# Three instead of four ordinary pairs ahead of the Strassen pairs in each feed-forward of a hybrid backbone step

## The reference, cut to what matters

```python
def swiglu(h, w_in, w_out):
    g, u = jnp.split(h @ w_in, 2, axis=-1)
    return (jax.nn.silu(g) * u) @ w_out

def trunk_layer(x, cond, ...):
    mod = (jax.nn.silu(cond) @ w_mod + b_mod)[:, None, :]
    sh1, sc1, g1, sh2, sc2, g2, sh3, sc3, g3 = jnp.split(mod, N_MOD, axis=-1)
    h = rms_norm(x, norm_pre[0]) * (1.0 + sc1) + sh1
    x = x + 0.5 * g1 * rms_norm(swiglu(h, ffn_w_in[0], ffn_w_out[0]), norm_post[0])
    h = rms_norm(x, norm_pre[1]) * (1.0 + sc2) + sh2
    m, s_f, s_b = mixer(h, ...)
    x = x + g2 * rms_norm(m, norm_post[1])
    h = rms_norm(x, norm_pre[2]) * (1.0 + sc3) + sh3
    x = x + 0.5 * g3 * rms_norm(swiglu(h, ffn_w_in[1], ffn_w_out[1]), norm_post[2])
```

## Time and profile before

| | us |
|---|---|
| runs before: median of 3 (lowest, highest) | 1409.32 (1406.62, 1411.38) |
| profiled execution, its own time | 1406.2 |
| its span, first to last instruction | 1404.3 |
| TensorE busy with matmuls | 1382.8 (98%) |
| VectorE busy | 720.4 (51%) |
| GpSimd busy | 716.1 (51%) |
| ScalarE busy | 580.5 (41%) |

### The profile page before, as it was taken

The page is one execution under the profiler, slowest core; times in us unless marked ns, Lnnn a source line. Parts: engine busy times, 40 slices in busy tenths (PEclk is TensorE's granted clock), DMA queues, the critical chain, the costliest instruction groups (busy, mean ns, idle before and its releaser), DMA issues.

```text
span 1404.3 us, 23518 instructions
## 1 busy us (share of the span) xinstructions
PE 1382.8 (98%) x9593; PEld 1264.8 (90%) x9593; DVE 720.4 (51%) x1082; ACT 580.5 (41%) x937; POOL 716.1 (51%) x528
## 2 busy tenths in 40 slices
PE   7999999999999999999999999999999999999998
PEld 5889899999788888999999999989999999988886
DVE  4635556666721431488786412135577666676033
ACT  6233333344634663234445222257344443354243
POOL 0464645465866681323223333552466555668663
PEclk9999999999999999999999999999999999999999
DMA  9747676232535551212112222333122223334465
GB/s 344 259 138 239 207 232 207 75 91 84 170 121 171 177 199 45 64 51 63 42 54 66 68 73 75 105 116 106 31 76 78 80 84 91 91 99 157 135 192 182
DMA packets 215294, 173.34 MB, mean 123 GB/s; under 512 B 6472, under 2 KB 175636, under 8 KB 215060
## 3 DMA queue, kind: packets, MB, share of 16 engines
q1 hardware_dynamic: 212448, 170.61, 39.1%
q10 hardware_dynamic: 2740, 1.24, 0.3%
HBM read 168.65 MB, written 3.17 MB: 122 GB/s over the span
## 4 chain that ended last, share of the span: by engine, by line
PE 93%; DVE 2%; DMA 1%; ACT 1%; POOL 1%; issue 1%; SPq 1%; ACTq 0%; DVEq 0%; POOLq 0%
PE PP L802 31%; PE PP L603 27%; PE PP L622 9%; PE PP L624 9%; PE PP L623 9%; PE PP L661 2%; PE PP L647 2%; PE PP L866 1%; DMA W_in<-in_ffn_w_out 1%; PE PP L992 1%; POOL W_lo L536 1%; PE PP L1008 1%; PE PP L1062 0%; DMA rowsB<-in_c_ctx 0%; PE PP L642 0%
## 5 line engine op out<-in xcount | busy, mean ns | idle before, releaser
L536 POOL TENSOR_TENSOR W_lo<-W_in,W_hi 128x512 fp32r<-128x512 f32 (+1 forms) x308 | 386.4, 1282 | 450.7 <-ACT W_hi L1200 441.1
L545 POOL TENSOR_TENSOR W_lo<-W_in,W_hi 128x512 fp32r<-128x512 f32 x108 | 169.7, 1585 | 190.5 <-ACT S_hi L1431 186.3
L1200 ACT ACTIVATE W_hi<-W_in 128x1024 fp32r<-128x1024 f32 x145 | 152.8, 1056 | 215.6 <-PE PP L624 121.2
L622 PE MATMUL PP<-W_hi,Mlo 128*128 128x512 f32 x440 | 172.3, 392 | 2.9 <-POOL W_lo L536 1.7
L624 PE MATMUL PP<-W_hi,Mhi 128*128 128x512 f32 x440 | 171.3, 389 | 0.0
L623 PE MATMUL PP<-W_lo,Mlo 128*128 128x512 f32 x440 | 171.2, 389 | 0.0
L603 PE MATMUL PP<-Hhi,W_hi 128*128 128x320 f32 (+2 forms) x640 | 154.1, 316 | 0.0
L603 PE MATMUL PP<-Hlo,W_hi 128*128 128x320 f32 (+2 forms) x640 | 149.7, 309 | 0.0
L603 PE MATMUL PP<-Hhi,W_lo 128*128 128x320 f32 (+2 forms) x640 | 149.5, 309 | 0.0
L802 PE MATMUL PP<-Hhi,W_hi 128*128 128x320 f32 x432 | 134.9, 312 | 0.5 <-DVE TT L1983 0.5
L802 PE MATMUL PP<-Hhi,W_lo 128*128 128x320 f32 x432 | 133.5, 309 | 0.0
(11 more groups left out here) (279 smaller groups left out, 2972.5 us busy)
## 6 DMA issues: line engine op xcount, KB each, us to landing
W_in<-in_ffn_w_out SPq DMA_DIRECT2D x176, 256.0 KB, 3.2
W_in<-in_ffn_w_in SPq DMA_DIRECT2D x83, 512.0 KB, 4.5
modl<-in_w_mod SPq DMA_DIRECT2D x14, 2048.0 KB, 8.2
W_in<-in_w_in SPq DMA_DIRECT2D x32, 512.0 KB, 3.8
modw<-in_w_mod SPq DMA_DIRECT2D x4, 2048.0 KB, 14.2
HL<-g_rows SPq DMA_DIRECT2D x6, 512.0 KB, 5.7
V_in<-in_w_in SPq DMA_DIRECT2D x10, 256.0 KB, 3.7
O_in<-in_w_out SPq DMA_DIRECT2D x10, 256.0 KB, 5.7
```

The lines of the kernel that those rows point to most:

```text
L536: return nc.gpsimd.tensor_tensor(lo[:, k0:k1, :], full[:, k0:k1, :], hi[:, k0:k1, :].bitcast(fp32), ALU.subtract)
L545: return nc.gpsimd.tensor_tensor(lo, full, hi.bitcast(fp32), ALU.subtract)
L622: mm(out, xh, wh, start=lead and kk == 0, stop=False)
L1200: A(W[i][0], W[i][2], ACT.Copy).then_inc(hi_done, 1)
```

## The change

`EARLY_PAIRS` becomes 3: each feed-forward does 3 ordinary and 19 Strassen pairs. Everything that was placed by pair moves with it.

- First feed-forward: the ordinary slabs 6 and 7 are gone. `MOD_AFTER` loses its last entry, so that three late modulation slabs come among the ordinary slabs and the fourth comes after the first Strassen pair. SP's queue there is rewritten: the first Strassen pair's value is loaded ahead of its gate, the gate waits for a modulation slab whose space it overlaps, then comes `next_mod(3)`, then the loop of the remaining pairs.
- The ring of four buffers of `in0s` is 12, 2, 0, 1 instead of 12, 1, 2, 0.
- Second feed-forward: `in1A` and `in1B` have 6 slabs instead of 8. The first Strassen pair's value takes buffer 9 (`I3`), which slab 6 of the ordinary ones had; the pairs behind it use 2, 0, 1, 12 in turn.
- ACT's `value_highs` and DVE's `first_sums`, `last_sum` and `lows` of the first Strassen pair come one ordinary pair earlier. In the second feed-forward DVE makes the token combinations after two ordinary products instead of three.

```diff
--- before.py
+++ after.py
@@ -27,7 +27,7 @@
 
 GROUP = ((0, 1, 2), (3, 4))
 G_COLS = ((0, 384), (384, 640))
-EARLY_PAIRS = 4
+EARLY_PAIRS = 3
 
 
 
@@ -46,23 +46,23 @@
 
 KEEP = [6, 7, 8, 9, 10]
 STAGES = [
-    ("in0", 2 * EARLY_PAIRS, [0, 1, 2, 11, 0, 1, 2, 0], False),
-    ("in0s", 2 * SEVEN, [12, 1, 2, 0], False),
+    ("in0", 2 * EARLY_PAIRS, [0, 1, 2, 11, 0, 1], False),
+    ("in0s", 2 * SEVEN, [12, 2, 0, 1], False),
     ("out0A", FT, [1, 2, 0, 3], False), ("out0B", FT, [0, 4, 5, 1, 2], False),
     ("vuA", 8, [6, 1, 7, 2, 8, 0, 9, 10], False), ("vuB", 8, [6, 1, 7, 2, 8, 0, 9, 10], True),
     ("heads", 4 * NH, [1, 2, 0], False),
     ("merge", 3 * KT, [2, 0, 1], False),
     ("woA", KT, KEEP[:3] + [2, 0, 1] + KEEP[3:], False),
     ("woB", KT, KEEP[:3] + [2, 0, 1] + KEEP[3:], True),
-    ("in1A", 2 * EARLY_PAIRS, KEEP[:2] + [2, 0, 1] + KEEP[2:], False),
-    ("in1B", 2 * EARLY_PAIRS, KEEP[:2] + [2, 0, 1] + KEEP[2:], True),
-    ("in1s", 2 * SEVEN, [12, 2, 0, 1], False),
+    ("in1A", 2 * EARLY_PAIRS, KEEP[:2] + [2, 0, 1] + KEEP[2:3], False),
+    ("in1B", 2 * EARLY_PAIRS, KEEP[:2] + [2, 0, 1] + KEEP[2:3], True),
+    ("in1s", 2 * SEVEN, [12, 9] + [2, 0, 1, 12] * SEVEN, False),
     ("out1A", FT, [2, 0, 1, 3], False), ("out1B", FT, [1, 4, 5, 2, 0], False),
 ]
 
 
 MOD_ROUNDS = ((0, 2), (1, 3))
-MOD_AFTER = [2, 3, 5, 7]
+MOD_AFTER = [2, 3, 5]
 EARLY_GATES = 3
 LAST = 3
 
@@ -121,10 +121,11 @@
     branch = base["merge"] + MERGE.index(("br", 3))
     for n, after in ((0, branch), (1, branch), (2, branch), (6, base["woA"] - 1), (7, base["woA"] - 1)):
         free[base["woA"] + n] = after
-    for n, after in ((0, base["woA"]), (1, base["woA"] + 1)) + tuple((n, base["in1A"] - 1) for n in (5, 6, 7)):
+    for n, after in ((0, base["woA"]), (1, base["woA"] + 1)) + ((5, base["in1A"] - 1),):
         free[base["in1A"] + n] = after
-    free[base["in0s"]] = 4
+    free[base["in0s"]] = 3
     free[base["in1s"]] = base["in1A"] - 1
+    free[base["in1s"] + 1] = base["in1A"] - 1
     return base, buf, free, order, need, fresh
 
 
@@ -204,6 +205,7 @@
             (tile_at(16), tile_at(38), tile_at(4), tile_at(4) + 8192, tile_at(4) + 2 * 8192))],
     }
     EXTRA = slab_buffer("W11", tile_at(14) - 8192)
+    KEPT["in1s"] = KEPT["in1A"]
     KEPT.update({"vuB": KEPT["vuA"], "woB": KEPT["woA"], "in1B": KEPT["in1A"]})
     SEVENTH = slab_buffer("W12", tile_at(34))
     ring_at = tile_at(34) + 8192
@@ -471,14 +473,18 @@
             sp.wait_ge(sem("mod_mm"), MOD_EARLY + (1 if i == 2 else i))
             load_mod(i)
 
-        for n in (4, 5, 6):
+        for n in (4, 5):
             load_in0(n)
         next_mod(2)
-        load_in0(7)
-        for p in range(SEVEN):
+        j = EARLY_PAIRS
+        load(BASE["in0s"] + 1, 0, KT, w0[:, :, DFF + j * P:DFF + (j + 1) * P])
+
+        sp.wait_ge(sem("mod_mm"), MOD_EARLY + 2)
+        load(BASE["in0s"], 0, KT, w0[:, :, j * P:(j + 1) * P])
+        next_mod(3)
+        for p in range(1, SEVEN):
             j = EARLY_PAIRS + p
-            load(BASE["in0s"] + 2 * p, 0, KT, w0[:, :, j * P:(j + 1) * P])
-            load(BASE["in0s"] + 2 * p + 1, 0, KT, w0[:, :, DFF + j * P:DFF + (j + 1) * P])
+            load_pair(BASE["in0s"] + 2 * p, w0, j)
             if 3 + p < MOD_LATE:
                 next_mod(3 + p)
         wo0 = ffn_w_out[0, 0].rearrange("(k p) n -> p k n", p=P)
@@ -569,8 +575,8 @@
         for n, i in enumerate(FRESH):
             if n < 3 or i in LO_DVE:
                 continue
-            if i in (6, BASE["out1A"]):
-                token_lows(int(i != 6))
+            if i in (BASE["out0A"], BASE["out1A"]):
+                token_lows(int(i == BASE["out1A"]))
             if i in (BASE["out0A"], BASE["out1A"]):
                 for p in range(SEVEN):
                     seven_low(int(i == BASE["out1A"]), p)
@@ -1486,7 +1492,6 @@
                 token_highs(0)
             if j == 2:
                 gate_highs(0, 0)
-            if j == 3:
                 value_highs(0, 0)
             after_slab(2 * j + 1)
         seven_gates(0)
@@ -1684,7 +1689,6 @@
                     token_highs(1)
                 if (grp, j) == (1, 1):
                     gate_highs(1, 0)
-                if (grp, j) == (1, 2):
                     value_highs(1, 0)
         seven_gates(1)
         out_group(2, 0)
@@ -2023,7 +2027,7 @@
             V.tensor_tensor(two(M32[:, j, :]), two(TT[0][:, :]), halves(1), ALU.mult).then_inc(sem("hid_ready"), 1)
             if j == 0:
                 token_combinations(0)
-            if j == 2:
+            if j == 1:
                 first_sums(0, 0)
                 last_sum(0, 0)
                 lows(0, 0)
@@ -2296,16 +2300,14 @@
         h_affine(1, 4)
         h_low(1, 4)
         early_hidden(0, 1)
+        token_combinations(1)
         early_hidden(0, 2)
-        token_combinations(1)
-        early_hidden(0, 3)
         early_hidden(1, 0)
-        early_hidden(1, 1)
         first_sums(1, 0)
         last_sum(1, 0)
+        early_hidden(1, 1)
+        lows(1, 0)
         early_hidden(1, 2)
-        lows(1, 0)
-        early_hidden(1, 3)
         seven_sums(1)
         first_group(2)
```

## The result

Before: 1409.32 us (median of 5 runs, 1406.62 to 1411.38). With the change: **1490.97 us** (median of 5, 1487.75 to 1493.29). Ratio 1.059, 95% interval 1.057 to 1.061: 82 us slower. The forecast was 1461 us in a range of 1448 to 1478. The direction was right and the range too low by 13 us. The profiled execution took 1492.4 us, against 1406.2 us before.

The account below looks back on a forecast made before the run. The kernel was taken to be bound by TensorE's matmuls. Terms -3.4 + 49.5 + 4.4 - 0.6 + 2.0 = +51.9 us on the median 1409.3 gave 1461 us, range 1448 to 1478.

Parts of the forecast that it names:

- Part 1: Both feed-forwards: one ordinary pair each becomes Strassen, taking 1.8 and 1.6 us of matmuls away, -3.4 us.
- Part 2: First feed-forward, Strassen pairs 0 to 10: loads behind the modulation slab delay `C22`, eleven waits of 4.5 us, +49.5 us.
- rival 2: Waits in the Strassen pairs halve TensorE's clock: 2.7 us a pair, 29 in all, 1490 us; in half of them 1475; chance 0.14.
- Part 3: First output slabs of the first feed-forward: slab 1's low 3.9 us later, ACT's late copies 0.5 more, +4.4 us.
- Part 4: Second feed-forward: DVE sums push back POOL's token lows at its head, +2.0 us; an output-slab wait goes, -0.6 us.
- Rivals 1: Pair loads served beside the modulation slab land in time, no eleven waits: 1411.5 us, chance 0.08; 1405.3 us, chance 0.02.
- Rival 3: Strassen pair loads later still, SP held up or every landing slow: 5.9 us a pair, 1476 us; chance 0.06.

Follow-up runs that it names:

- the version without the side effects: Changed kernel with pair loads ahead of the modulation slab, ring 0, 1, 2, 12 after the first pair, hidden tile 3 split early with tiles 0 to 2: 1403.35 us.
- the other ring: Changed kernel with pair loads ahead of the modulation slab, and first feed-forward Strassen slab ring 0, 1, 2, 12 after the first pair: 1411.8 us, ratio 1.0016.

## Why the prediction was wrong, step by step

**Part 1, the matmuls (-3.4 us): right as far as shown.** The pairs of the second feed-forward grew by 12.4 us, one pair's worth, and the version without the side effects is 4.3 us (2.8 to 6.6 by its interval) below the kernel before.

**Part 2, the loads (49.5 us): mechanism, place and number right, size a little low.** Eleven waits, 53.8 us. Nine of them are 4.5 to 4.8 us, the other two 5.6 and 6.2. In those two the modulation slab landed in 8.0 us, as the median does, but DVE's first sum began 12.6 and 12.8 us after its issue instead of 11.5, because the second weight slab landed 12.5 and 12.7 us after it. Why that slab was slower there is open. The wait of 5.6 us lies inside part 2's bounds, that of 6.2 above.

**The step that failed is the dismissal of rival 2,** "the waits are half as long as that idle time", which gave it a chance of 0.14 and kept its full price, 1490, out of the range. It was the case: the clock fell in or just behind all eleven waits. Its price in the pairs was about 20 us by the trace (22.7 with the two small terms named above) and 15.9 by the run with forty transposes, in which one low stretch stayed, against the 29 that rival 2 worked out. I had one row on the clock, from an idle stretch of 9.3 us, and took its length for evidence on shorter ones, which it is not. The Trainium skill, "TensorE: Matmul & The Clock Gate", section "Part 1: The HAM clock gate", spoke against this change by its rule that idle time throttles the array. The trace agrees: the granted clock was 0.92 over each of the three pairs shown.

**Part 3, the first output slabs (4.4 us, bounds 2 and 6): the wait right, its size wrong by its own bounds.** The wait for slab 1's low was 3.8 us, 3.4 more than before (0.37). Three things came on top. The clock fell behind it: TensorE worked for 5.5 us at half rate, 2.7 us. A wait of 4.3 us for a hidden tile's hi part, where 0.8 stood before, and a second low stretch of 3.4 us behind it, 1.7 us. The sum is 11.4. The runs agree: the other ring took 5.1 us off and the early split another 6.5, each version held against the kernel before beside it, 11.6 together. I had let ACT be "two copies late" and had not followed which tiles it splits, and when. ACT is where that second wait arose:

```profile
460.16 1.06 ACT L1206 ACTIVATE W_hi<-W_in 128x1024 fp32r<-128x1024 f32 x1 [6.66 <-DMA W_in<-in_ffn_w_out]
461.12 1.35 ACT L1342 ACTIVATE Mlo<-M 128x640 fp32r<-128x640 f32 x2
```

The tiles stand in ACT's queue behind a copy that waits 6.66 us for its load. Why that load is so late (SP spent 4.1 us on the mask's, `YB`, just ahead, against 2.5 before) was not tried.

**Part 4, the second feed-forward (+2.0 and -0.6): the contention right, its effect smaller.** From the first matmul of `in1A` to the end of the span it takes 435.4 us before and 435.7 after. The three sums that now fall beside POOL's lows of the tokens took 3.4 us each:

```profile
1087.58 3.35 DVE L1921 TENSOR_TENSOR S_in<-S_in,W_in 128x512 f32<-128x512 f32 x1
1090.85 3.45 DVE L1922 TENSOR_TENSOR I_in<-W_in,I_in 128x512 f32<-128x512 f32 x1
1094.21 3.45 DVE L1932 TENSOR_TENSOR S_in<-W_in,S_in 128x512 f32<-128x512 f32 x1
```

while POOL's three lows took 9.82 us in place of 8.80, 1.0 more and not the 2.0 of the forecast. TensorE waited 0.85 us. The wait of 0.66 us at the first output slab went, as forecast; but two waits for a hidden tile's hi part came, 0.63 and 0.31 us, where none stood, the first of them here:

```profile
1350.17 0.50 PE L628 MATMUL PP<-W_hi,Mlo 128*128 128x512 f32 x1 [0.63 <-DVE Mhi L1963]
```

The balance is near zero, as the sum of part 4 and its share of part 1 (2.0 - 0.6 - 1.6) had it, but that is in part luck: the terms are 0.85, +0.3 and -1.6, and 0.7 us have no row here.

**The sum.** In the trace: -3.4 forecast for matmuls; 53.8 waits; 22.7 low clock in the pairs, with the two small terms; 11.4 at the first output slabs; 0.85 at the second head and 0.3 at the second output slabs; together 85.7 of 86.0. The difference to the forecast's 51.9 is the clock in the pairs, about 60% of it, then part 3 (7.0) and the longer waits (4.3).

**Rivals 1 and 3.** The loads did not come in time: 10.3 us from issue to landing, median. Rival 3's sign was seen, SP took 3.8 to 4.4 us in nine of the first ten pairs, 2.0 in the other, to issue the two weight slabs with the modulation's 2 MB in flight:

```profile
109.91 0.37 SPq L431 DMA_DIRECT2D modl<-in_w_mod  x1
110.32 4.15 SPq L417 DMA_DIRECT2D W_in<-in_ffn_w_in  x2
```

where they took 2.13 and 0.99. But in this pair DVE's sum could start 11.5 us after the modulation load, the forecast's time, so the slow issue cost nothing more.

## What to carry to other kernels

When a loop's head start shrinks by one, look for every queue in which "wait for item i-1" stands ahead of something unrelated. Here an earlier place for a load, one line up, was worth 74 us, and most of that was an operation which TensorE needed (`C22`) standing in DVE's queue behind one that waited for the load. Price a wait on TensorE with the clock: behind a wait of 4.9 us in every turn the work was slower too, by 2 us a turn. And when tiles change from one kind to the other, follow the side work (splits, copies) that is placed by kind, since one tile's split in the wrong place was worth 6.5 us or more.

## What the runs showed of the hardware

- The clock fell in waits much shorter than expected. Of the waits of 4.5 to 6.2 us all eleven lowered it, and so did the one of 3.8 us. Around 2 us it went both ways: it fell behind single waits of 1.95, 1.97, 2.08 and 2.70 us and behind seven of the eight of 2.2 to 2.5 us for `C22` in the run with 20 transposes, and held through single ones of 1.81, 2.25, 2.28, 2.33 and 2.42 us. In the pairs of the run with `C22` first, waits of 1.0 to 1.6 us left it at 1.00.
- Forty small transposes in the wait held the clock at 1.00 over the 180 us in which it was at 0.90 without them; twenty left it at 0.90.
- DVE's sums of 128x512 in float32 took 0.68 us alone and 3.35 to 3.45 us while POOL made lows of 128x1280, three in a row, and POOL took 9.82 us in place of 8.80.
- A modulation slab of 2 MB landed in 8.0 us (7.9 to 8.2), two weight slabs of 512 KB right behind it in 9.3 to 11.7 us each; issued apart from it they take 3.6 to 5.0 us.
